# Sliding-window attention: sink logits written into fixed PSUM columns by ScalarE, the rotary half swap and cosine moved to VectorE

## The reference

```python
z = h @ w_in                                   # queries, keys, values of both groups
# rope, per head of 64 (half = 32)
x1, x2 = xf[..., :half], xf[..., half:]
out = concatenate([x1 * cos - x2 * sin, x2 * cos + x1 * sin])
# sink_attention
s = einsum(q, k) * 64 ** -0.5;  s = where(mask, s, -inf)
m = maximum(max(s), sink)
e = exp(s - m)
p = e / (sum(e) + exp(sink - m))
o = einsum(p, v)
```

## Time and profile before

| | us |
|---|---|
| median of three runs | 2799.26 |
| lowest, highest | 2795.54, 2804.72 |
| the profiled execution: its time | 2802.72 |
| the profiled execution: its span, first to last instruction | 2801.2 |
| TensorE busy in the span | 2675.9 |
| VectorE busy | 1782.4 |
| ScalarE busy | 1137.6 |
| GpSimd busy | 226.1 |

### The profile page before, as it was taken

The page is one execution under the profiler, slowest core; times in us unless marked ns, Lnnn a source line. Parts: engine busy times, 40 slices in busy tenths (PEclk is TensorE's granted clock), DMA queues, the critical chain, the costliest instruction groups (busy, mean ns, idle before and its releaser), DMA issues.

```text
span 2801.2 us, 48529 instructions
## 1 busy us (share of the span) xinstructions
PE 2675.9 (96%) x19589; PEld 2591.4 (93%) x19589; DVE 1782.4 (64%) x2285; ACT 1137.6 (41%) x1632; POOL 226.1 (8%) x318
## 2 busy tenths in 40 slices
PE   6799999999989978899999999989999999999998
PEld 6678899999979978899999999989999999999998
DVE  7544434334463458777777777678888888887622
ACT  4344434333451135455555555423333333334421
POOL 0200012111200000100000000110000000000000
PEclk8899999999999989999999999989999999999999
DMA  4111122222212223455444544786654666331321
GB/s 167 47 40 35 37 83 81 79 77 74 83 35 90 76 76 113 186 190 190 181 179 179 180 179 179 264 313 220 217 175 134 207 209 209 99 109 66 105 98 56
DMA packets 217737, 372.41 MB, mean 133 GB/s; under 512 B 17472, under 2 KB 149440, under 8 KB 216128
## 3 DMA queue, kind: packets, MB, share of 16 engines
q1 hardware_dynamic: 178144, 211.34, 23.6%
q0 software_dynamic: 37776, 156.98, 14.9%
q10 hardware_dynamic: 1616, 1.18, 0.1%
HBM read 288.49 MB, written 80.94 MB: 132 GB/s over the span
## 4 chain that ended last, share of the span: by engine, by line
PE 66%; DVE 16%; issue 8%; ACT 7%; DMA 3%; ACTq 0%; SPq 0%; POOL 0%; DVEq 0%
PE tile L530 29%; PE misc L572 14%; PE tile L572 12%; DVE o_lo L1702 6%; PE misc L787 3%; ACT o_hi L959 2%; PE misc L530 2%; DMA raw<-in_w 1%; DVE raw L1724 1%; ACT f_blk L1232 1%; PE misc L767 1%; DVE raw L1730 1%; ACT c_blk L1255 1%; DVE x_lo L1799 1%; DVE c_blk L1754 1%
## 5 line engine op out<-in xcount | busy, mean ns | idle before, releaser
L959 ACT ACTIVATE o_hi<-raw 128x1024 fp32r<-128x1024 f32 x434 | 459.5, 1060 | 682.4 <-PE tile L572 196.0
L1702 DVE TENSOR_TENSOR o_lo<-raw,o_hi 128x1024 fp32r<-128x1024 f32 x434 | 531.4, 1224 | 248.7 <-ACT o_hi L959 248.2
L530 PE MATMUL tile<-x_hi,w_hi 128*128 128x288 f32 (+1 forms) x2080 | 473.9, 310 | 19.7 <-DVE x_lo L1624 6.7
L530 PE MATMUL tile<-x_hi,w_lo 128*128 128x288 f32 (+1 forms) x2080 | 449.3, 298 | 0.0
L530 PE MATMUL tile<-x_lo,w_hi 128*128 128x288 f32 (+1 forms) x2080 | 448.7, 298 | 0.0
L572 PE MATMUL misc<-dop,o_hi 128*128 128x288 f32 x2048 | 415.6, 297 | 8.6 <-DVE acc L1774 5.0
L572 PE MATMUL tile<-t_r,o_hi 128*128 128x288 f32 x1920 | 397.7, 302 | 26.1 <-ACT c_blk L959 7.4
L530 PEld LDWEIGHTS tile<-x_hi,w_hi 128*128 128x128 f32 (+1 forms) x2080 | 332.9, 190 | 46.8 <-issue 38.8
L572 PEld LDWEIGHTS tile<-t_r,o_hi 128*128 128x128 f32 x1920 | 313.1, 192 | 37.3 <-issue 30.4
L572 PEld LDWEIGHTS misc<-dop,o_hi 128*128 128x128 f32 x2048 | 331.1, 189 | 9.3 <-issue 6.5
L530 PEld LDWEIGHTS tile<-x_lo,w_hi 128*128 128x128 f32 (+1 forms) x2080 | 336.6, 190 | 1.2
(11 more groups left out here) (270 smaller groups left out, 3877.8 us busy)
## 6 DMA issues: line engine op xcount, KB each, us to landing
w_raw<-in_w SPq DMA_DIRECT2D x146, 512.0 KB, 3.5
raw<-in_w SPq DMA_DIRECT2D x512, 128.0 KB, 2.9
dop<-hid_operands POOLq DMA_DIRECT2D x56, 1152.0 KB, 8.4
raw<-in_w SPq DMA_DIRECT2D x120, 512.0 KB, 5.4
hid_operands<-x_hi POOLq DMA_DIRECT2D x31, 1008.0 KB, 7.2
hid_operands<-x_lo POOLq DMA_DIRECT2D x31, 1008.0 KB, 9.4
acc<-in_x SPq DMA_DIRECT2D x4, 1152.0 KB, 9.4
h_rows<-acc POOLq DMA_DIRECT2D x4, 1152.0 KB, 5.1
```

What stands on the lines that cost most here:

```text
L530: ins = nc.tensor.matmul(dst[:, h, :], w, x[:, h * HALF:(h + 1) * HALF], start=first and a == 0, stop=last and a == 2)
L959: return nc.scalar.activation(out, in_, func, scale=scale)
L1702: V.tensor_tensor(o_lo[g % 3][:, :], raw[n % 2][SOURCE[s]][:, :], o_hi[g % 3][:, :], ALU.subtract)\
```

## The change

Four things, all in the sliding attention.

- The sink logit of a block is no longer written by TensorE. It now has a fixed column for each head (column 1 for head 0, 258 for head 1, in both halves of the score tile); the block's keys lie behind the one and ahead of the other. ScalarE copies the two heads' logits into the four columns (two copies of 128x2) once a pair, behind the last output copy of the pair before, and TensorE's slot 0 waits for that (`sinks_set`).
- The half swap is no longer a product on TensorE. VectorE multiplies `z_t` by the cosine (128x576) and, in four instructions of 32 partitions that read one quarter and write its neighbour, by the sine; then it subtracts.
- The cosine product leaves GpSimd. The projection's PSUM tile is given free as soon as `z_t` is copied.
- Every slot stands one chunk later: slot 0 at chunk 7, slot 9 at chunk 0 of the next tile.

```diff
-SWA_SLOTS = {c: c - 6 for c in range(6, 21)}
+SWA_SLOTS = {c: c - 7 for c in range(7, 22)}
+SINK_A, SINK_B = 1, 258
 # span
-        return 512 * (j % 2), 1 + (128 if qt == 0 else 256 if qt < 4 else WIN + SAMPLE)
+        keys = 128 if qt == 0 else 256 if qt < 4 else WIN + SAMPLE
+        return 512 * (j % 2) + (SINK_A if head == 0 else SINK_B - keys), 1 + keys
 # TensorE, attend
+                        if kind == "swa":
+                            pe.wait_ge(sinks_set, lin(pair + 1, i, dp))
...
-                        end = at + span(kind, j)[1]
-                        ins = nc.tensor.matmul(scores_ps[:, end - 1:end], ident[:, :], sink_col(pair, head, i, dp),
-                                               start=True, stop=True)
 # TensorE, rotate
-                pe.wait_ge(z_ready, lin(r + 1, i, dr))
-                for h in range(2):
-                    ins = nc.tensor.matmul(tile_ps(n)[:, h, :], swap[:, :], z_t[:, h * HALF:(h + 1) * HALF], start=True, stop=True)
-                ins.then_inc(swapped, 1)
 # ScalarE
+            def sinks_in(pair, i=None, dp=0):
+                copy(sink_places(0), sink_col(pair, 0, i, dp))
+                copy(sink_places(1), sink_col(pair, 1, i, dp)).then_inc(sinks_set, 1)
...
-                    act.wait_ge(swapped, lin(att + 1, i, dp))
-                    act.wait_ge(cos_done, lin(att + 1, i, dp))
+                    act.wait_ge(turned_z, lin(5 * att + 5, i, 5 * dp))
                     copy(halves(z_t[:, :]), tile_ps(T_QA + att)).then_inc(z_ready, 1)
 # VectorE
+            def turn(r, n, i=None, dr=0):
+                out = rot if r else k_rot
+                dve.wait_ge(z_ready, lin(r + 1, i, dr))
+                if r:
+                    dve.sem_inc(tile_free[n % 2], 1)
+                    dve.wait_ge(op_dve, lin(OP_KV + 2 * r - 2, i, 2 * dr))
+                V.tensor_tensor(out[:, :], z_t[:, :], cos_t[:, :], ALU.mult).then_inc(turned_z, 1)
+                for a, b in ((0, 32), (32, 0), (64, 96), (96, 64)):
+                    V.tensor_tensor(rot2[a:a + 32, :], z_t[b:b + 32, :], sin_t[b:b + 32, :], ALU.mult).then_inc(turned_z, 1)
 # VectorE, rotate
-                V.tensor_tensor(halves(rot2[:, :]), tile_ps(n), halves(sin_t[:, :]), ALU.mult).then_inc(free, 1)
-                dve.wait_ge(cos_done, lin(r + 1, i, dr))
...
-                V.tensor_tensor(out[:, :], out[:, :], rot2[:, :], ALU.add).then_inc(rot_ready, 1)
+                V.tensor_tensor(out[:, :], out[:, :], rot2[:, :], ALU.subtract).then_inc(rot_ready, 1)
 # VectorE, swa_part
+                if c == 1:
+                    turn(att + 1, T_QA + att, i, dp)
 # GpSimd
-                P.tensor_tensor((rot if r else k_rot)[:, :], z_t[:, :], cos_t[:, :], ALU.mult).then_inc(cos_done, 1)
```

More of the change, by code:

```diff
@@ L426, in sink_col, with sink_places @@
             if i is None:
-                return sinks[:, 2 * pair + head:2 * pair + head + 1]
-            return sinks[:, bass.ds(i * (2 * dp) + (2 * pair + head), 1)]
+                return sinks[:, 2 * pair + head:2 * pair + head + 1].to_broadcast([128, 2])
+            return sinks[:, bass.ds(i * (2 * dp) + (2 * pair + head), 1)].to_broadcast([128, 2])
+        def sink_places(head):
+            at = (SINK_A, SINK_B)[head]
+            return scores_ps.rearrange("p (b c) -> p b c", b=2)[:, :, at]
         def settle(eng):
@@ L763, in attend @@
                         settle(pe)
-                    cols_ = key_cols(kind, qt)
+                    cols_ = key_cols(kind, qt, head)
                     for k, col in enumerate(cols_):
@@ L790, in attend, with key_cols @@
                     ins.then_inc(weighed, 1)
-            def key_cols(kind, qt):
+            def key_cols(kind, qt, head):
                 if kind == "swa":
-                    return [0] if qt == 0 else [0, 128]
+                    first = 1 - head
+                    return [first] if qt == 0 else [first, first + 128]
                 return [128 * k for k in range(qt + 1)]
@@ L827, in swa_between @@
                     swa_rest(c, pair - 1, i, dp)
-                if c == 1:
-                    rotate(pair + 1, T_QA + pair, i, dp)
-                if c == 6:
+                if c == 7:
                     pe.wait_ge(op_dve, lin(OP_KV + 2 * pair + 2, i, 2 * dp))
-                if c >= 6:
+                if c >= 7:
                     attend("swa", SWA_SLOTS[c], pair, i, dp)
@@ L1022, in attend @@
                         copy(dst[:, PROMPT:TOK], scores_ps[:, 512 - SAMPLE:512]).then_inc(out_free, 1)
+                        if kind == "swa" and (i is not None or pair < PAIRS - 1):
+                            sinks_in(pair + 1, i, dp)
+            def sinks_in(pair, i=None, dp=0):
+                copy(sink_places(0), sink_col(pair, 0, i, dp))
+                copy(sink_places(1), sink_col(pair, 1, i, dp)).then_inc(sinks_set, 1)
             act.sem_inc(exp_done, 2)
@@ L1027, in _ @@
             act.dma_start(ident_f[:, :], t["ident"]).then_inc(ident_landed, 16)
-            for dst, name in ((cols, "cols"), (cos_t, "cos"), (sin_t, "sin"), (swap, "swap"), (win_f, "win"),
+            for dst, name in ((cols, "cols"), (cos_t, "cos"), (sin_t, "sin"), (win_f, "win"),
                               (tri_f, "tri"), (sinks, "sinks"), (bf, "bf"), (ck_t, "swa_ck"), (cv_t, "swa_cv_t")):
@@ L1124, in fox_pair @@
                         ahead.upto(U_FOX + 6 * q + c // 8 + 2, i, 6 * dp)
-                    if att is None and c <= KT + 4:
+                    if att is None and c <= KT + 5:
                         swa_part(c, PAIRS - 1)
@@ L1920, in _ @@
             pool.dma_start(f_row(F_C, PAST), t["clogf"]).then_inc(clogf_landed, 16)
-            def cosine(r, i=None, dr=0):
-                pool.wait_ge(z_ready, lin(r + 1, i, dr))
-                P.tensor_tensor((rot if r else k_rot)[:, :], z_t[:, :], cos_t[:, :], ALU.mult).then_inc(cos_done, 1)
-            cosine(0)
-            lanes_free(cos_done, 1)
             kk = slice(0, TOK)
@@ L1931, in _ @@
             pool.wait_ge(rot_ready, 1)
-            cosine(1)
             pool.wait_ge(va_out, 1)
@@ L1947, in _ @@
             pool.wait_ge(f_saved, 16 * 13)
-            def cosine_after(r, i=None, dr=0):
-                pool.wait_ge(op_dve, lin(OP_KV + 2 * r - 2, i, 2 * dr))
-                cosine(r, i, dr)
-            with pool.Fori(0, 7) as i:
-                cosine_after(2, i, 1)
             def zeros(first, parts):
```

34 lines of the change are left out of this document (15 added, 19 removed).

## The result

| | before | after |
|---|---|---|
| median | 2800.88 (9 runs) | 2813.39 (9 runs) |
| lowest, highest | 2794.66, 2805.91 | 2806.20, 2816.92 |
| ratio, 95% interval | | 1.0043, 1.0029 to 1.0057 |
| profiled execution: time, span | 2802.72, 2801.2 | 2813.63, 2812.1 |

A forecast was written before the change was run, and what follows sets the result against it. TensorE, busy 96% of the span, was taken as the bound. Tiles +1.8, tail +2.4 and front 0 sum to +4.2 on the profiled 2802.72, giving 2807, or 2803 us for the median; range 2791 to 2815.

The forecast's parts named there:

- the case that had 0.17: Whole kernel: slower by more than 0.3%, 8.4 us, through a falling clock or longer waits; chance 0.17.
- the forecast case: Whole kernel: TensorE's gain and the new waits balance, no change beyond 0.3%, 8.4 us; chance 0.75.
- Wait of 1.0, of 1.2, of 0.7 us: TensorE in chunks 1, 3 and 4 of a tile: waits for block 6's copy, block 9's scaling and block 9's copy.
- A quarter product of 0.79 us, five of them 3.95: VectorE's cosine and sine products: 0.79 us from start to start, run end to end, 3.95 us, at least 3.4.
- Period 30.4 us: One sliding-attention tile on TensorE, start to start: 13.8 us to slot 0 plus 16.6, against 29.80 before.
- The waits of chunk 10 keep their size, may grow by 0.1 to 0.2.: TensorE's waits in chunk 10: 0.87 us together, perhaps 0.1 to 0.2 more since TensorE gets there sooner.
- Sinks of 1.58 us a pair: TensorE's sink products: removing ten a pair, at 0.14 or 0.23 us each, takes 1.58 us off its row.
- Tail "+2.4": Behind the last pair: 1.4 us more work from slot 9 and a 1.0 us wait behind `w_lo`, +2.4 us.
- Front "0, from -2 to +3": At the kernel's front, a longer chain for keys and first queries but cover behind it: 0 charged, -2 to +3 us.
- some 3.5 us later for a slot one chunk further: First pair's slot 0, waiting for VectorE's query lows (105.25 before): some 3.5 us later, one chunk (0.8 us) further on.
- I take +0.3 us a tile: Six tiles with a rotation: +0.3 us each, bounds -0.3 and +0.8, +1.8 us in all.
- the mechanism as a rival: Chunks 1 to 4: waits make TensorE's clock fall, 2 to 3 us a tile, +17, giving 2820 us; chance 0.07.

The follow-up runs named there:

- experiment 4: Changed kernel reordered: chunk-0 weight unit split later, block 9's scaling ahead of the five products, its copy ahead of the query copies; 2780.94 us, 0.9934 of the kernel before.
- experiment 6: Changed kernel with one move, ScalarE's copy of block 9 ahead of its two query copies; 2807.56 us, 1.0036 of the kernel before.
- experiment 7: Changed kernel with one 128-partition sine product in place of four over 32, for timing only (results not the layer's); 2781.29 us, 0.9935 of the kernel before.
- experiment 9: Changed kernel with only block 9's scaling and copy put ahead, chunk-0 weight unit not moved; 2786.45 us, 0.9953 of the kernel before.
- experiment 1: Kernel before with only the sink part of the change, slots and rotation as before; 2794.44 us, 0.9981 of the kernel before.
- experiment 3: Changed kernel with idle TensorE products into unread columns ahead of chunks 1, 3 and 4; 2808.57 us, 1.0031 of the kernel before.
- experiment 8: Changed kernel without its sink part, TensorE writing the sink logits as before; 2817.97 us, 1.0068 of the kernel before.
- experiment 10: Changed kernel with sinks on ScalarE and rotation on VectorE, but slots where they were (slot 0 at chunk 6); 2795.79 us, 0.9987 of the kernel before.
- experiment 5: The kernel of experiment 4 with the other weight unit split at chunk 5 instead of 8; 2770.57 us, 0.9908 of the kernel before.
- experiment 2: Kernel before with every slot one chunk later and nothing else; 2802.70 us, 1.0008 of the kernel before.

## Why the prediction came out as it did

The forecast was 2803 us, with 0.75 on no change of more than 0.3%; the kernel is slower by 0.43%, the case that had 0.17. The time lies inside the range, near its upper end, which allowed for "part of a clock loss"; that is no credit to the forecast case, which had none.

- *"Wait of 1.0, of 1.2, of 0.7 us" in chunks 1, 3 and 4.* Right in place and cause, and within some 0.2 us in size: 0.82 to 0.90, 1.23 to 1.39, 0.49 to 0.50 (the last absent in two of the tiles that lost clock). T+3.2, T+8.3, T+10.6 and slot 0 at T+13.6 stand against T+3.2, T+8.3, T+10.7 and T+13.8 of the forecast. Experiments 4, 6, 7 and 9 take the waits away one by one by the order or the product that I blamed.
- *A quarter product of 0.79 us, five of them 3.95.* Measured 3.91 together. The rule of the Trainium skill's page "VectorE: DVE Perf Modes", section "Two Vector instructions with no wait between them", holds: the quarters run end to end, while two products on all 128 partitions in experiment 7 stand 0.68 us apart with 0.76 of length, overlapping.
- *"Period 30.4 us", taken as 30.1.* At full clock 29.98 and 29.97, up to 30.07: right.
- *"The waits of chunk 10 keep their size, may grow by 0.1 to 0.2."* 1.04 to 1.07 us in place of 0.87 (0.84 in one tile that lost clock): right for the change. Experiment 1 shows the general case, which I would have got wrong: TensorE time taken ahead of a chain's fixed end becomes wait, 0.68 us a tile there, of the 1.95 taken.
- *Sinks of 1.58 us a pair.* Too low: experiment 1 has TensorE busy 26.97 us in a period of 28.52, against 28.92 in 29.80 before, 1.95 less. The head's first block, "taken at 0.14", has 0.19 in the trace (213.27 to 213.46); the rest of the difference stays open.
- *The ends.* Tail "+2.4": measured +2.4. Front "0, from -2 to +3": measured -1.4, of which 0.5 is there when ScalarE's wait for the gate rows ends (141.54 against 142.08); the rest comes in the tile behind it, and was not taken apart. There "some 3.5 us later for a slot one chunk further": 107.81 against 105.25, 2.6.
- *"I take +0.3 us a tile", +1.8 for six.* Measured +10.3. This is the term that failed, and by the clock: at full clock it is +1.3 to +1.5. I had the mechanism as a rival, with its place ("chunks 1 to 4 would hold waits"), its size ("2 to 3 us a tile"; measured 1.5 to 2.6) and its sign to look for ("any tile's clock under 1.00"), and gave it 0.07, against it one row: waits of 0.54 and 0.33 leave the clock at 1.00. That row says nothing of waits that are three times as long in sum. The step from 0.9 us of idle time to 2.9 in nine was an extrapolation, and a chance near a half would have been more honest. Its "seven times" was four in six.

So +4.2 became 4.2 - 1.4 (front) - 0.3 (tiles at full clock by experiment 3, 1.5 for 1.8) + 8.8 (clock) = 11.3 in the profile, of 10.9 measured; the medians have 12.5. Experiments 3 (fill the waits) and 1, 6, 8 and 10 (other waits, the same fall) show the clock term, and experiments 4 and 5 that nothing in the work removed or added had to cost anything.

**What stays open:** which of two tiles with equal waits loses its clock. 0.82, 1.32 and 0.49 us in succession left it alone at 175 to 183 and cost it 1.5 us behind those at 238 to 246; the runs here don't tell what differs.

## What to carry to other kernels

When work moves from the bounding engine to an idle one, walk the idle engine's program row by row: the price is what then stands behind the new rows (here one scaling, one copy and one maximum, 3 us a tile), and it is had back by reordering, not by moving work again. Give a slot's chain first place and put weight splits and long products into the chunks where no maximum or scaling is due. Waits of about 1 us that come in pairs on a TensorE that is otherwise full are to be priced with the clock's fall on top of their length: 1.3 to some 3 us in a tile that had one, and three to six tiles of six had one.

## What the runs showed of the hardware

- **Short waits cost clock.** Two, up to 5.2 us apart, did it: 0.90 and 1.39 (the change), 1.05 and 0.50 (experiment 1), 0.83 and 1.31 (experiment 6), 0.61 and 1.33 (experiment 8). Of six tiles it came in four, three, six and six. These did not in any tile: 0.54 and 0.33 (before), 0.61 to 0.69 and 0.36 fourteen us away (experiment 2), 0.86 and 0.2 with 0.82 to 0.90 thirteen us away (experiments 7 and 9). A fall lasted 3.4 us at half clock in experiment 1 (0.28 and 0.29 short over 3 us each) and 6.8 in the change.
- **A scaling beside GpSimd's product is four times as long.** VectorE's `TENSOR_SCALAR` of block 9 in the kernel before, and GpSimd's cosine product beside it:

```profile
205.38 1.27 DVE L1444 TENSOR_SCALAR s_p<-s_p,stat 128x193 f32<-128x193 f32 x1
```

```profile
205.04 1.50 POOL L1924 TENSOR_TENSOR rot<-z_t,cos_t 128x576 f32<-128x576 f32 x1 [28.30 <-ACT z_t L959]
```

  The scaling ends when GpSimd's product does (206.65 and 206.54); elsewhere it takes 0.32. In the change, without that product, all twelve between 160 and 350 us take 0.32:

```profile
L1445 DVE TENSOR_SCALAR s_p<-s_p,stat 128x193 f32<-128x193 f32 x12 | 3.9, 322 | 0.4
```

  The kernel before shows both: 1.27 in each of the six tiles with GpSimd's product beside the scaling, 0.32 behind the last pair, where there is no rotation. It cost nothing before, since TensorE did not wait for it there. The Trainium skill's page "SBUF — State Buffer", section "Who interferes with whom", says that VectorE's `tensor_scalar` in its two-port form and a GpSimd instruction shut each other out for a whole instruction; the two rows agree in the order and the end (0.11 us apart, less than the scaling's own 0.32, so not to the last tenth).
- **A product over 32 partitions is as long as one over 128**: 749 ns in the mean of 24 against 758 of the six with the cosine.
